# Eleven gate pairs with both halves of the activations in one product and seven rotating banks, and a score block packed into another's bank

## What is computed

```
u = rmsnorm(x, g_mix)
proj = u @ w_in                      # 2048 x 11264; its last 2 x 2048 columns are the branch gates A and B
q, k = rmsnorm(heads(sb_q)), rmsnorm(heads(sb_k))
z = (q @ k.T) * scale                # per head, strictly causal
log_keep = where(strict, log_sigmoid(-z), 0)
later = cumsum_from_the_right(log_keep) - log_keep
y_a = exp(log_sigmoid(z) + later) @ v
m = sigmoid(gate_A) * (y_a @ p_a) + sigmoid(gate_B) * (y_b @ p_b)
h = x + m @ w_o
out = h + ConvFFN(rmsnorm(h))
```

## Time and profile before

| | before |
|---|---|
| median of 3 runs | 2773.16 us (2772.32 to 2773.98) |
| the profiled execution: its own time / span | 2772.84 us / 2771.3 us |
| PE busy | 2766.9 us, 14838 matmuls |
| DVE busy | 2112.9 us |
| ACT busy | 1279.5 us |
| POOL busy | 430.7 us |
| chain that ended last | PE 99%, DVE 1% |
| gate pairs (L2278, L2279, L2280) in that chain | 3% each |

### The profile page before, as it was taken

How to read it: one execution, slowest core, us unless ns; L and a number is a source line. 1 busy time by engine, 2 the same in 40 slices (tenths; PEclk the granted TensorE clock), 3 DMA queues, 4 the chain that set the end, 5 groups by cost and what they waited for, 6 DMA issues and landing times.

```text
span 2771.3 us, 41246 instructions
## 1 busy us (share of the span) xinstructions
PE 2766.9 (100%) x14838; PEld 2404.0 (87%) x14838; DVE 2112.9 (76%) x3547; ACT 1279.5 (46%) x1743; POOL 430.7 (16%) x579
## 2 busy tenths in 40 slices
PE   9999999999999999999999999999999999999999
PEld 7888888888889999888889988888888888888888
DVE  7776777677777778444468988888888888888884
ACT  5444444444333344333345555555555554555554
POOL 2022154234400000000100110111101111110112
PEclk9999999999999999999999999999999999999999
DMA  5464586666535555444455666666656666666667
GB/s 177 149 179 104 170 200 140 172 185 128 111 119 159 168 171 182 138 143 144 141 169 142 149 140 141 137 137 145 135 139 137 142 141 135 143 135 139 138 144 164
DMA packets 187447, 410.98 MB, mean 148 GB/s; under 512 B 22288, under 2 KB 50320, under 8 KB 186128
## 3 DMA queue, kind: packets, MB, share of 16 engines
q1 hardware_dynamic: 120240, 283.90, 33.3%
q0 software_dynamic: 67040, 124.82, 24.5%
HBM read 347.81 MB, written 112.72 MB: 166 GB/s over the span
## 4 chain that ended last, share of the span: by engine, by line
PE 99%; DVE 1%; ACT 0%; issue 0%; POOL 0%; DVEq 0%; POOLq 0%
PE bank L2325 17%; PE bank L2042 12%; PE bank L2044 12%; PE bank L2043 12%; PE bank L2331 9%; PE bank L2422 6%; PE bank L2425 6%; PE bank L2421 6%; PE bank L2278 3%; PE bank L2280 3%; PE bank L2279 3%; PE bank L2386 2%; PE bank L2388 2%; PE bank L2387 2%; PE bank L2116 1%; PE bank L2106 0%
## 5 line engine op out<-in xcount | busy, mean ns | idle before, releaser
L993 ACT ACTIVATE w_hi<-w_two 128x896 fp32r<-128x896 f32 (+1 forms) x528 | 433.0, 838 | 451.4 <-DVE w_two L1787 404.5
L1794 DVE TENSOR_TENSOR w_lo<-w_two,w_hi 128x896 fp32r<-128x896 f32 (+1 forms) x528 | 496.6, 952 | 88.4 <-ACT w_hi L993 88.3
L2325 PE MATMUL bank<-v_parts,w_hi 128*128 128x512 f32 x2072 | 503.8, 391 | 0.0
L2325 PEld LDWEIGHTS bank<-v_parts,w_hi 128*128 128x128 f32 x2072 | 379.6, 188 | 72.7
L2042 PE MATMUL bank<-u_hi,w_hi 128*128 128x512 f32 x1000 | 395.0, 395 | 0.2 <-DVE w_lo L1161 0.2
L2044 PE MATMUL bank<-u_hi,w_lo 128*128 128x512 f32 x1000 | 389.9, 390 | 0.0
L2043 PE MATMUL bank<-u_lo,w_hi 128*128 128x512 f32 x1000 | 389.3, 389 | 0.0
L687 POOL DMA_DIRECT2D out_t<-stage x168 | 142.6, 851 | 1158.7 <-ACT stage L1065 1129.9
L1161 DVE TENSOR_TENSOR w_lo<-w_raw,w_hi 128x1024 fp32r<-128x1024 f32 x189 | 230.3, 1222 | 115.3 <-ACT w_hi L705 113.2
L2331 PEld LDWEIGHTS bank<-v_parts,w_lo 128*128 128x128 f32 x2072 | 268.1, 191 | 11.5
L2331 PE MATMUL bank<-v_parts,w_lo 128*128 128x256 f32 x2072 | 271.7, 283 | 0.0
(11 more groups left out here) (310 smaller groups left out, 5253.1 us busy)
## 6 DMA issues: line engine op xcount, KB each, us to landing
w_two<-wslots SPq DMA_DIRECT2D x504, 256.0 KB, 2.7
w_raw<-wstream SPq DMA_DIRECT2D x189, 512.0 KB, 3.5
out_t<-stage POOLq DMA_DIRECT2D x168, 256.0 KB, 4.7
sums_scratch<-wfirst POOLq DMA_DIRECT2D x72, 448.0 KB, 5.7
g_raw<-sums_scratch SPq DMA_DIRECT2D x48, 448.0 KB, 3.3
g_raw<-wgates SPq DMA_DIRECT2D x48, 256.0 KB, 2.9
w_two<-sums_scratch SPq DMA_DIRECT2D x24, 448.0 KB, 3.3
sums_scratch<-sums_scratch POOLq DMA_DIRECT2D x72, 128.0 KB, 4.5
```

The lines of the kernel that those rows point to most:

```text
L993: act.activation(w4_hi[ring][:, 0:width], w4_raw[ring][:, 0:width], ACT.Copy).then_inc(w4_hi_ready, 1)
L1794: dve.tensor_tensor(w4_lo[ring][:, 0:width], w4_raw[ring][:, 0:width], w4_hi[ring][:, 0:width].bitcast(F32), ALU.subtract).then_inc(w4_rea ...
L2325: return nc.tensor.matmul(bank[j].rearrange("p (a c) -> p a c", a=2), w4_hi[ring][:, w * P:(w + 1) * P], both, start=kp == 0, stop=kp == K ...
```

## The change

1. **Eleven wide pairs.** Pairs 0 to 10 (`WIDE_PAIRS = 11`) take each of the seven products with one matmul of 512 columns (`gate_highs`, high weights by both halves of the activations, which now lie in one tensor `u_both` or `t_both`) and one of 256 (`gate_lows`), 14 matmuls in a slot for 21. Each product has a bank of its own. The order in a slot depends on its place: even slots take the highs first, odd ones the lows; slot 0 of a pair is split 4 / 3 (`SPLIT`), slot 7 is split 3 / 4 (`EARLY`).
2. **Seven rotating banks.** `gate_banks(k)` starts one bank lower with each pair. Product 0 of a pair goes to the bank that the pair before left free; product i goes to the bank of product i - 1 of the pair before and waits until it is copied.
3. **Copies.** ACT copies each of the seven banks (128x512) to `g_parts` in SBUF (`gate_copy`), after `gate_hi(j + 2)` in the last step of a pair. DVE adds the low halves there (`wide_early`, `wide_late`), and combines from SBUF (`wide_pair`).
4. **The last pair** is computed as before, by `gate_slot`, in the rotated banks; its products wait for the copies of pair 10.
5. **Scores.** The fourth score block moves to the free 128 columns of the second one's bank, so that three instructions in place of four do for the absolute value on ACT, for `sp` on DVE and for each half's product with `ntri_r` on PE.

```diff
+WIDE_PAIRS = GATE_PAIRS - 1
+SPLIT = 4
+GATE_STEPS = 7
...
+    g_parts = sb("g_parts", 2 * KT * SEQ, R1)
...
+    def z_row(b):
+
+        return (Z[0][:, :], Z[1][:, 0:3 * P], Z[2][:, 2 * P:SEQ], Z[1][:, 3 * P:SEQ])[b]
...
-    def gate_bank(k):
-
-        return 4 * ((k + 1) % 2)
+    def gate_banks(k):
+
+        return [(2 - k + j) % 8 for j in range(7)]
...
             def gate_p1(k):
                 act.wait_ge(unit_done, gate_unit(k))
-                if k > 0:
-                    act.wait_ge(tile_out, 2 + TILES_G + GATE_TILES + 2 * k)
...
+            def gate_copy(k):
+                act.wait_ge(gate_step, GATE_STEPS * k)
+                for c, b in enumerate(gate_banks(k)):
+                    if c < 6:
+                        act.wait_ge(early_done, 6 * k + c + 1)
+                    else:
+                        act.wait_ge(unit_done, gate_unit(k))
+                    act.activation(g_parts.rearrange("p (a x) -> p a x", a=2)[:, :, 2 * c * SEQ + HALF:2 * c * SEQ + SEQ],
+                                   bank[b].rearrange("p (a c) -> p a c", a=2), ACT.Copy).then_inc(p1_ready, 1)
...
             for j in range(PAIR_SLOTS):
-                if j > 0 and j % KP == 0:
-                    gate_p1(j // KP - 1)
...
+                if j % KP == KP - 1 and j // KP < WIDE_PAIRS:
+                    gate_copy(j // KP)
...
+            def wide_early(k):
+
+                dve.wait_ge(p1_ready, gate_copies(k) + EARLY)
+                dve.tensor_tensor(gate_high(0, EARLY), gate_high(0, EARLY), gate_low(0, EARLY),
+                                  ALU.add).then_inc(gate_step, 1)
+
+            def wide_late(k):
+
+                done = GATE_STEPS * k
+                dve.wait_ge(p1_ready, gate_copies(k) + 7)
+                dve.tensor_tensor(gate_high(EARLY, 7 - EARLY), gate_high(EARLY, 7 - EARLY), gate_low(EARLY, 7 - EARLY),
+                                  ALU.add).then_inc(gate_step, 1)
+                dve.wait_ge(gate_step, done + 1)
+                dve.tensor_tensor(gate_low(0), gate_high(1), gate_high(0), ALU.subtract).then_inc(gate_step, 1)
...
+            def wide_pair(k, q):
+
+                done, stores = GATE_STEPS * k, 16 * ((GATE_TILES + 2 * k) // 2)
+                two = lambda t: t.rearrange("p (a c) -> p a c", a=2)
+                if q == 1:
+                    dve.wait_ge(gate_step, done + 3)
+                    dve.tensor_tensor(gate_low(1), gate_low(0), gate_high(2), ALU.subtract).then_inc(gate_step, 1)
+                    dve.scalar_tensor_tensor(out=gate_high(1), in0=gate_high(4), scalar=-1.0, in1=gate_low(0),
+                                             op0=ALU.mult, op1=ALU.subtract).then_inc(gate_step, 1)
+                    dve.wait_ge(gate_stored[1], stores)
+                    dve.wait_ge(gate_step, done + 4)
+                    dve.tensor_tensor(two(g_out[1][:, :]), gate_low(1).unsqueeze(1).broadcast_to((P, 2, HALF)),
+                                      gate_high(3, 2), ALU.add).then_inc(gate_step, 1)
+                if q == 2:
+                    dve.wait_ge(gate_stored[0], stores)
+                    dve.wait_ge(gate_step, done + 5)
+                    dve.tensor_tensor(two(g_out[0][:, :]), gate_high(5, 2), gate_high(0, 2),
+                                      ALU.add).then_inc(gate_step, 1)
+                if q > 1:
+                    dve.wait_ge(gate_step, done + (7, 6)[q - 2])
+                    dve.tensor_tensor(g_out[q - 2][:, :], g_out[q - 2][:, :], r_tok[:, :],
                                       ALU.mult).then_inc(tile_out, 1)
...
+                k, q = j // KP - 1, j % KP
+                if k >= 0 and q == 0:
+                    wide_early(k)
+                    gate_sums(j + 3)
+                    wide_late(k)
...
-                if j >= KP and j % KP < 5:
-                    gate_pair(j // KP - 1, j % KP)
+                if k >= 0 and 0 < q < 4:
+                    wide_pair(k, q)
...
-                        for b in range(NB):
-                            nc.tensor.matmul(by_blocks(Z[b][:, b * P:SEQ]), ntri_r[:, :], keys_row(part, b),
+                        for (_, z, n), (x, width) in zip(z_banks(), own_blocks(part)):
+                            nc.tensor.matmul(in_blocks(z, width), ntri_r[:, :], x,
                                              start=False, stop=True, skip_group_check=True)
...
+            def gate_highs(j, i0, i1):
+
+                k, kp = divmod(j, KP)
+                for i in range(i0, i1):
+                    w, x = WIDE_PRODUCTS[i]
+                    if kp == 0 and k == 0 and i == 6:
+                        pe.wait_ge(tile_out, 2 + TILES_G + GATE_TILES - 1)
+                    if kp == 0 and k == 1 and i == 0:
+                        pe.wait_ge(tile_out, 2 + TILES_G + GATE_TILES)
+                    if kp == 0 and k > 0:
+                        pe.wait_ge(p1_ready, gate_copies(k - 1) + i)
+                    ins = nc.tensor.matmul(bank[gate_banks(k)[i]].rearrange("p (a c) -> p a c", a=2),
+                                           blocks(g_hi[j % PLACES], w), gate_moving(kp, x), start=kp == 0,
+                                           stop=kp == KP - 1, skip_group_check=True)
+                    if kp == KP - 1 and i < 6:
+                        ins.then_inc(early_done, 1)
+                return ins
...
+            def gate_wide(j):
...
+                pe.wait_ge(w_hi_ready, n + 1)
+                if kp == 0:
+                    gate_highs(j, 0, SPLIT)
+                    pe.wait_ge(w_ready, n + 1)
+                    gate_lows(j, 0, SPLIT)
+                    gate_highs(j, SPLIT, 7)
+                    ins = gate_lows(j, SPLIT, 7)
+                elif kp == KP - 1:
+                    pe.wait_ge(w_ready, n + 1)
+                    gate_lows(j, 0, EARLY)
+                    gate_highs(j, 0, EARLY)
+                    gate_lows(j, EARLY, 7)
+                    ins = gate_highs(j, EARLY, 7)
```

More of the change, by code:

```diff
@@ L827, in head_steps @@
                     act.wait_ge(z_masked, per(1, 1))
-                    for b in range(NB):
-                        ins = act.activation(za[:, ROW[b]:ROW[b + 1]], Z[b][:, b * P:SEQ], ACT.Abs)
+                    for at_, z, n in z_banks():
+                        ins = act.activation(za[:, at_:at_ + n], z, ACT.Abs)
                     steps.did(ins)
@@ L2156, in head_steps @@
                     for b in range(rounded):
-                        key, out = slice(b * P, (b + 1) * P), Z[b][:, b * P:SEQ]
-                        nc.tensor.matmul(out, kn_hi[:, key], qn_hi[:, b * P:SEQ], start=True, stop=False)
-                        nc.tensor.matmul(out, kn_hi[:, key], qn_lo[:, b * P:SEQ], start=False, stop=False)
+                        key, out = slice(b * P, (b + 1) * P), z_row(b)
+                        nc.tensor.matmul(out, kn_hi[:, key], qn_hi[:, b * P:SEQ], start=b == 0, stop=False,
+                                         skip_group_check=True)
+                        nc.tensor.matmul(out, kn_hi[:, key], qn_lo[:, b * P:SEQ], start=False, stop=False,
+                                         skip_group_check=True)
                     if rounded:
@@ L2259, in gate_slot @@
                 n = START_P + j
-                b0 = gate_bank(k)
-                if kp == 0:
-                    if k == 0:
-                        pe.wait_ge(ms_ready, 3 * HEADS)
-                    else:
-                        pe.wait_ge(tile_out, 2 + TILES_G + GATE_TILES + 2 * (k - 1))
-                if k == 0:
-                    pe.wait_ge(t_kp_ready, kp + 1)
+                b = gate_banks(k)
                 pe.wait_ge(w_ready, n + 1)
                 even, odd = 2 * kp * SEQ, (2 * kp + 1) * SEQ
-                for w, x, b, half in PRODUCTS:
-                    out = bank[b0 + b][:, half * HALF:(half + 1) * HALF]
+                for w, x, i, half in PRODUCTS:
+                    if kp == 0 and half == 0:
+                        pe.wait_ge(p1_ready, gate_copies(k - 1) + i)
+                    out = bank[b[i]][:, half * HALF:(half + 1) * HALF]
                     wh, wl = (blocks(t[j % PLACES], w) for t in (g_hi, g_lo))
@@ new lines, in gate_lows @@
+            def gate_lows(j, i0, i1):
+                k, kp = divmod(j, KP)
+                for i in range(i0, i1):
+                    w, x = WIDE_PRODUCTS[i]
+                    ins = nc.tensor.matmul(bank[gate_banks(k)[i]][:, 0:HALF], blocks(g_lo[j % PLACES], w),
+                                           gate_moving(kp, x)[:, 0, :], start=False, stop=False, skip_group_check=True)
+                return ins
+            def gate_wide(j):
+                k, kp = divmod(j, KP)
+                n = START_P + j
+                if j == 0:
+                    pe.wait_ge(ms_ready, 3 * HEADS)
+                if k == 0:
+                    pe.wait_ge(t_kp_ready, kp + 1)
+                pe.wait_ge(w_hi_ready, n + 1)
[11 more added lines that the diff above has]
```

(10 more changed lines are left out.)

104 lines of the change are left out of this document (61 added, 43 removed).

## The result

The changed kernel takes 2777.26 us (median of 22 runs, 2774.74 to 2779.22), the kernel before 2773.22 us beside it: ratio 1.0015, 95% interval 1.0009 to 1.0021. That is 0.15% slower, inside "no change" as the prediction bounded it, but by 4 us and not by the forecast 0.5. The profiled execution has a span of 2775.0 us and a time of its own of 2776.54; before, 2771.3 and 2772.84.

What follows compares the result with a forecast made beforehand. PE bounded the kernel before; with the change a DVE and ACT ring would set gate pairs. 2772.84 + 0.8 (gate stage) - 0.3 (scores) = 2773.3 us profiled, so 2773.7 us predicted, range 2768 to 2779 us.

Steps and rivals of the forecast that it cites:

- the ring: Gate stage: the instruction order of DVE and ACT closes a loop not through PE, 20.3 us a pair; chance 0.73.
- outer rivals: Gate pairs: PE stays the bound, 2766.0 us, chance 0.15; or ACT's copies do not overlap, 2780 us, chance 0.12.
- PE's saving: Gate stage, wide pairs: 19.48 us against 20.16, so 0.68 us a pair if PE waited for nothing, 7.5 in eleven.
- PE stays the bound: Gate pairs: ring 0.8 us shorter than summed, no copy waited for, PE's 7.5 us arrive; 2766.0 us, chance 0.15.
- PE's waits: First slot of a gate pair: PE waits for ACT's copies at products 2, 3 and 6, 0.8 us a boundary.
- pair 0: First gate pair: waits for no copy, so 0.7 us is gained.
- pairs 2 to 10: Gate pairs in the steady state: nine at 20.27 us against 20.16, together +1.0 us.
- pair 11: Last gate pair, computed as before: PE waits for g_lo, +0.7 us; 0.1 may go at the stage's end.
- pair 1: Second gate pair: comes before the ring has closed, some 0.2 us less wait, -0.1 us.
- The scores: Heads' score blocks: three matmuls for four per head and half, taken as -0.3 us in all.
- the landing of the loads: Gate stage, 256 KB loads: landing 2.9 us after issue, 0.3 us slack; 0.4 us later would cost some 2 us.
- unknown costs: Gate stage: copies' distance (0.45 us gives some -1.5 us, 0.51 gives +2) and late 256 KB loads (some 2 us).

Runs made afterwards that it cites:

- e5_nosums: Changed kernel with the odd slots loading the even slot's 448 KB as they are and DVE's gate_sums left out (wrong weights); 2765.64 us, ratio to before 0.9972.
- e3_raw4: Changed kernel with a fourth buffer for raw gate weights from slot 12 on, so each load is issued one slot earlier; 2773.82 us, ratio to before 1.0003.
- e1_scores: Kernel before with only the new place of the fourth score block, gate pairs as before; 2772.77 us, ratio to before 0.9998.
- e9_shift56: Changed kernel with 56 waits on a long-reached semaphore at the start of PE's program; 2779.17 us, ratio to before 1.0020.
- e2_gates: Kernel before with only the eleven wide gate pairs, score blocks as before; 2779.94 us, ratio to before 1.0024.
- e4_copy8: Changed kernel with ACT copying the last bank twice, an eighth copy into unused columns; 2781.52 us, ratio to before 1.0032.
- e6_order: Changed kernel with ACT making the first two of seven copies ahead of the g_hi that stood before them all; 2774.38 us, ratio to before 1.0004.
- e7_order_inter: As e6_order, and the last slot's 14 matmuls go product by product so banks 0 and 1 complete earlier; 2773.62 us, ratio to before 1.0000.

## Why the prediction was right, and where its size was off

"Same" and the range of 2768 to 2779 us hold, and the ring is the mechanism that the runs show. But the ring with its own bounds gave 2771 to 2777 us, and 2777.26 lies just above that: it is inside the stated range because this was widened halfway to the outer rivals. The stage, forecast 0.5 to 1.5 us longer, is 4.9 us longer.

- **PE's saving, 0.68 us a pair.** Right: e5_nosums has pairs of 19.50 us for 20.16 before, 0.66 us. That is 56 matmuls less at 11.8 ns each. An estimate from the Trainium skill's 2.5 ns of fixed part (TensorE: Matmul & The Clock Gate, "Wait — 56ns, not 53.3ns?") would have been 0.14 us a pair; the measurement decides for the rows.
- **The ring of 20.3 us.** Right to 0.02 us: 20.29, and its change by one copy (0.48) and by two orders came out as summed. Both outer rivals fall with it: pairs of 19.5 us (PE stays the bound) appear only where DVE is relieved, and the seven copies take 3.51 us together, 0.49 us apart, not 0.58.
- **PE's waits.** Right: in e3_raw4 PEld waits 9.6 us for copies at ten boundaries, 0.9 us at each but the first. The pair is 0.78 us longer than PE's own 19.50, for 0.8 forecast, and the copies start right behind a `g_hi`.
- **Without late loads** the stage is 1.7 us longer than before (e3_raw4), forecast 0.8. From the first product of each pair to that of the next, and against before: pair 0 gives -0.6 us (forecast -0.7), pairs 2 to 10 together +1.1 (+1.0), pair 11 with the stage's end +0.5 (+0.6). The term that is off is pair 1: 20.79 us, +0.6, where I had -0.1. PEld waits 1.5 us for copies at the first boundary; I had put less wait there than later. The median of e3_raw4, 2773.82 us, is my 2773.7 to 0.1 us, which is luck in part: its stage is 0.9 us longer than summed, and in its profile the stage starts 0.8 us earlier than before, where I had 0.3.
- **The scores, -0.3 us.** e1_scores agrees, but cannot tell 0.3 us from nothing.
- **The term that was mis-sized is the landing of the loads.** I held it at nothing in the sum and at "some 2 us in all" among the unknown costs, for the 256 KB loads alone. It measured 3.4 us (the change against e3_raw4). Two things were missing. The load that waits cost most for is the 448 KB one, whose slack I had not worked out: it has 3.5 us against a median landing of 3.3. And I went by a median where the tail decides: single loads take up to 5.4 us. Before, no wait of PE came from them. In the ring it depends on where the late load falls: in pair 2 a wait of 1.46 us made the pair 1.41 us longer, in pair 9 one of 1.06 us made it 0.19 longer.

## What to carry to other kernels

When a change fills a helper engine up to the pair's length, write down the loop that the order of the engines' instructions closes before counting PE's gain: here it gave 20.3 us to 0.02. In such a loop every transfer that the loop itself releases needs slack for its slowest landing, not for its median; one more buffer brought back 3.4 us, and moving two copies ahead of a rounding that they did not depend on shortened the loop by 0.2 us a pair, 0.44 with a reordered last slot.

## What the runs showed of the hardware that was not expected

- Instruction fetches of 16 KB stand in the trace among the DMA packets of the data (queue q8; in the stretch shown one packet, counted at 1.6% of the 16 engines' time). Loads of 448 KB that had one among them took up to 5.4 us in the change, 6.2 us in e9_shift56, for a median of 3.3; in the change all nine loads of 4.2 us and more had a fetch among them.
- Adding waits that do nothing to PE's program, 56 or 160 at its very start, moved those fetches and the long pairs of a stage 830 us later. That the scores and the gates do not add (-0.3 and +6.8 us alone, +4.0 together) fits this: the long waits for loads in the first and last pair of e2_gates each have a fetch among the loads. No run shows it by itself.
- A single wait of PE can be followed by half its clock: 1.30 us idle in e2_gates, 1.48 in e4_copy8 and 1.94 in e6_order were each followed by some 3.4 us at 1.2 GHz. Yet 2.26 us idle in e9_shift56 (up to 919.51), 1.43 in the last pair of e4_copy8, 1.39 and 1.37 in e7_order_inter and 1.09 in the change were not. The length of the wait does not tell these apart; what does stays open.
